# A hybrid decoder layer on one core: the sample's NSA attention moves into the block of the NSA merge, and the scan's decay product moves to GpSimd

## The reference

```python
cum = jnp.cumsum(dt * a, axis=2)
seg = cum_t[..., :, None] - cum_t[..., None, :]
decay = jnp.exp(jnp.where(causal, seg, -jnp.inf))
cb = jnp.einsum('bcign,bcjgn->bcgij', cm, bm)
xdt = xh * dt[..., None]
y_diag = jnp.einsum('bcgeij,bcjgep->bcigep', cb[:, :, :, None] * decay, xdt)
states = jnp.einsum('bcjgn,bcjgep->bcgepn', bm, xdt * decay_end[..., None])
```

```python
s_s = jnp.einsum('bqkgd,bkqmd->bkgqm', qb, k_sel) * scale     # likewise s_c (compressed), s_w (window)
p_s = masked_softmax(s_s, ...)
o_s = jnp.einsum('bkgqm,bkqmd->bqkgd', p_s, v_sel)
o_nsa = (gb[..., 0:1] * o_c + gb[..., 1:2] * o_s + gb[..., 2:3] * o_w) @ w['w_nsa_o']
mixed = gm[:, :, 0] * o_ssd + gm[:, :, 1] * o_nsa + gm[:, :, 2] * o_mem
```

## Time and profile before

| | |
|---|---|
| median of 3 runs | 1879.28 us |
| profiled execution | 1881.37 us, span 1879.4 us |
| mean granted TensorE clock | 0.951 |
| TensorE busy | 1697.0 us (90%) |
| VectorE busy | 949.1 us (51%) |
| ScalarE busy | 704.8 us (38%) |
| GpSimd busy | 662.6 us (35%) |

### The profile page before, as it was taken

One profiled execution on the slowest core, in us unless ns is written; L12 is line 12 of the kernel. 1 busy time (PEld: TensorE's weight loads), 2 busy tenths in 40 slices (PEclk: granted clock), 3 DMA queues, 4 the chain that ended last, 5 costly groups with the idle time before them and its releaser, 6 DMA issues. The chain is left out here.

```text
span 1879.4 us, 33817 instructions
## 1 busy us (share of the span) xinstructions
PE 1697.0 (90%) x13060; PEld 1542.2 (82%) x13060; DVE 949.1 (51%) x1543; ACT 704.8 (38%) x1502; POOL 662.6 (35%) x346
## 2 busy tenths in 40 slices
PE   6999995786997999879997799989998799999999
PEld 5999993455997999536665699988797799999999
DVE  4476766996611352157773313552223568777300
ACT  3333336884611331145551233333412333333221
POOL 2344434663343333125441243011143244444443
PEclk9999998888999999879998899999998899999999
DMA  4223216442222432230003323644423222232233
GB/s 141 69 89 91 95 60 211 169 145 101 79 90 70 147 103 94 94 108 28 1 0 96 118 91 113 225 135 168 180 89 124 61 86 89 91 95 93 70 93 119
DMA packets 60239, 193.65 MB, mean 103 GB/s; under 512 B 6934, under 2 KB 19734, under 8 KB 56726
## 3 DMA queue, kind: packets, MB, share of 16 engines
q1 hardware_dynamic: 58838, 190.30, 30.5%
q10 hardware_dynamic: 1312, 2.14, 0.3%
HBM read 174.47 MB, written 22.14 MB: 105 GB/s over the span
## 5 line engine op out<-in xcount | busy, mean ns | idle before, releaser
L254 POOL TENSOR_TENSOR mm_ring<-mm_raw,mm_ring 128x1024 fp32r<-128x1024 f32 x94 | 229.0, 2438 | 487.9 <-ACT mm_ring L231 364.2
L264 PE MATMUL up_pp<-h,mm_ring 128*128 128x260 f32 x2016 | 244.0, 284 | 3.0 <-POOL mm_ring L254 3.0
L264 PEld LDWEIGHTS up_pp<-h,mm_ring 128*128 128x128 f32 x2016 | 243.8, 189 | 3.2 <-ACT up_conv_s L2850 3.2
L231 ACT CAST mm_ring<-mm_raw 128x1024 fp32r<-128x1024 f32 x106 | 111.1, 1049 | 335.1 <-PE up_pp L264 231.0
L264 PE MATMUL ssd_pp<-h,ssd_ring 128*128 128x260 f32 x1920 | 233.8, 285 | 3.0 <-POOL ssd_ring L254 3.0
L264 PEld LDWEIGHTS ssd_pp<-h,ssd_ring 128*128 128x128 f32 x1920 | 233.2, 190 | 3.2 <-ACT gates_raw L515 3.2
L264 PE MATMUL up_pp<-act_t,mm_ring 128*128 128x260 f32 x1344 | 165.7, 286 | 7.5 <-POOL mm_ring L254 7.5
L264 PEld LDWEIGHTS up_pp<-act_t,mm_ring 128*128 128x128 f32 x1344 | 165.3, 192 | 7.9 <-issue 7.9
L254 POOL TENSOR_TENSOR ssd_ring<-mixed,ssd_ring 128x1024 fp32r<-128x1024 f32 x42 | 102.4, 2440 | 170.0 <-ACT ssd_ring L231 153.6
L264 PE MATMUL nq_pp<-h,nq_ring 128*128 128x260 f32 x960 | 122.5, 289 | 10.4 <-POOL nq_ring L254 10.4
L264 PEld LDWEIGHTS nq_pp<-h,nq_ring 128*128 128x128 f32 x960 | 119.5, 192 | 11.3 <-issue 10.5
(11 more groups left out here) (424 smaller groups left out, 3103.3 us busy)
## 6 DMA issues: line engine op xcount, KB each, us to landing
mm_raw<-in_w_up SPq DMA_DIRECT2D x44, 512.0 KB, 3.7
mixed<-in_w_ssd SPq DMA_DIRECT2D x42, 512.0 KB, 3.5
mem_ring<-in_mem_kv SPq DMA_DIRECT2D x16, 1024.0 KB, 6.0
ms_raw<-in_w_ssd_merge SPq DMA_DIRECT2D x24, 512.0 KB, 3.5
mm_raw<-in_w_mkv_qm SPq DMA_DIRECT2D x24, 512.0 KB, 3.7
nq_raw<-in_w_qk SPq DMA_DIRECT2D x20, 512.0 KB, 3.7
sc_seg<-cum_rows SPq DMA_DIRECT2D x16, 512.0 KB, 4.9
mixed<-in_ssd_state SPq DMA_DIRECT2D x16, 512.0 KB, 4.2
```

The costliest lines, as they stand in the source:

```text
L231: act.copy(self.ring[:, b % 2, 0], self.raw[:, b % 2]).then_inc(self.high, 1)
L254: pool.tensor_tensor(self.ring[:, u, 1], self.raw[:, u], self.ring[:, u, 0].bitcast(F32), ALU.subtract).then_inc(self.low, 1)
L264: last = pe.matmul(out(n), self.ring[:, b % 2, wn, k], x[:, xn, chunk + k, part], start=start and k == 0 and wn + xn == 0, stop=stop and k ...
```

## The change

**Scan.** The step size dt goes into the exponent: log_dt_cum = ln(max(dt, 2e-38)) - cum takes the place of minus cum as the bias, at the price of a logarithm on ScalarE and one more instruction on VectorE, each once, in the projection before the scan. The eight scaled copies of x become one plain copy (sc_xt), and C times B is copied to SBUF beside B turned. GpSimd forms m from SBUF (mix). TensorE waits for GpSimd before the products with m, and SP waits for GpSimd before it reloads sc_seg.

The diff, cut to its core:

```diff
@@ StepSizes.dve_all / act_d
-        do(dve.tensor_scalar(negcum[:], cum[:], -1.0, None, ALU.mult))
+        do(dve.tensor_scalar(log_dt_cum[:], dtr[:], TINY, None, ALU.max))
...
+        do(dve.tensor_tensor(log_dt_cum[:], log_dt_cum[:], cum[:], ALU.subtract))
...
-        act.activation(self.dend[:], self.dend[:], ACT.Exp).then_inc(self.exped, 1)
+        act.activation(self.dend[:], self.dend[:], ACT.Exp)
+        act.activation(self.log_dt_cum[:], self.log_dt_cum[:], ACT.Ln).then_inc(self.exped, 1)
@@ scan, SP
-                    sp.wait_ge(ready, v + 1)
+                    sp.wait_ge(mixed_up, v + 1)
                     load_rows(v + AHEAD)
@@ scan, GpSimd
+            def mix(v):
+                pool.wait_ge(taken, v + 1)
+                pool.wait_ge(exped, v + 1)
+                if v >= 2:
+                    pool.wait_ge(multiplied, v - 1)
+                pool.tensor_tensor(m[:, v % 2], seg[:, v % AHEAD], br[:, v % 2, 0, :].unsqueeze(1).broadcast_to(
+                    [P, HPG, P]), ALU.mult).then_inc(mixed_up, 1)
...
             diagonals(1)
+            mix(0)
             for v in range(STEPS):
                 if v:
                     gate(v - 1)
                 scale(v)
+                if v + 1 < STEPS:
+                    mix(v + 1)
                 if v + 2 < STEPS:
                     hide_future(v + 2)
@@ scan, TensorE
                 if v:
                     pe.wait_ge(gained, v)
+                pe.wait_ge(mixed_up, v + 1)
                 for e in range(HPG):
-                    mm = pe.matmul(pyd[:, e, :], m[:, v % 2, e, :], xdt[:, v % 2, e, :], start=True, stop=True)
+                    mm = pe.matmul(pyd[:, e, :], m[:, v % 2, e, :], xt[:, v % 2, e, :], start=True, stop=True)
@@ scan, ScalarE
-                act.copy(br[:, v % 2, :], pcb[:, 1, :])
-                for e in range(HPG):
-                    ins = act.activation(xdt[:, v % 2, e, :], px[:, e, :], ACT.Copy,
-                                         scale=dtr[:, k, g * HPG + e:g * HPG + e + 1])
-                ins.then_inc(taken, 1)
+                act.copy(br[:, v % 2], pcb[:, 0:2, :])
+                act.copy(xt[:, v % 2], px[:]).then_inc(taken, 1)
@@ scan, VectorE
                 dve.wait_ge(taken, v + 1)
-                dve.tensor_tensor(xend[:, v % 2], px[:], of_heads(wend, v), ALU.mult)
-                dve.wait_ge(exped, v + 1)
-                dve.tensor_tensor(m[:, v % 2], seg[:, v % AHEAD], pcb[:, 0, :].unsqueeze(1).broadcast_to(
-                    [P, HPG, P]), ALU.mult).then_inc(ready, 1)
+                dve.tensor_tensor(xend[:, v % 2], px[:], of_heads(wend, v), ALU.mult).then_inc(ready, 1)
@@ merge_nsa, SP
+            piece(2)
+            sp.wait_ge(scored, 1)
+            keys(0)
+            piece(3)
+            keys(1)
+            piece(4)
+            sp.wait_ge(valued, 1)
+            values(0)
+            piece(5)
+            values(1)
+            for q in range(6, KC + 2):
+                piece(q)
+                if q == 7:
+                    sp.wait_ge(valued, 2)
+                if q >= KC:
+                    part = slice((q - KC) * HALF_K, (q - KC + 1) * HALF_K)
+                    sp.dma_start(mem[:, part], d["mem"][:, part]).then_inc(mem_landed, 16)
@@ merge_nsa, TensorE
+            def gates(t):
+                if t:
+                    pe.wait_ge(gated, t)
+                w.multiply(pe, t // 2, t % 2, lambda m: banks[:, gate_banks(t) + m, 0:HALF], h, 0, HALF_PARTS)
+            def scores(b):
+                if b:
+                    pe.wait_ge(k_landed, 32)
+                pe.wait_ge(q_ready, b + 1)
+                for n in range(2):
+                    for ch in range(2):
+                        for strip in range(STRIPS):
+                            q = 2 * strip + n
+                            mm = pe.matmul(psc[STRIP * strip:STRIP * (strip + 1), 0:PAST + 1], qd[:, ch, q, :],
+                                           kt[:, ch, q, :], start=n == 0 and ch == 0, stop=n == 1 and ch == 1, ...)
...
+            scores(0)
+            gates(0)
...
+            turn_weights(0)
+            gates(1)
+            values(0)
+            scores(1)
+            gates(2)
+            turn_weights(1)
+            gates(3)
+            values(1)
...
+            gates(4)
+            pe.wait_ge(o_done, 1)
+            pe.transpose(pot, osum[:], ident[:]).then_inc(o_turned, 1)
+            for t in range(PLAIN + 1, KC):
+                gates(t)
+            pe.wait_ge(low, KC + 1)
+            for t in range(KC):
...
@@ merge_nsa, ScalarE and GpSimd, end of the block
-            following.write_first_ahead(act)
+            following.write_first_after(act, w)
...
+            for b in range(2):
+                following.write_low_of(pool, 0, b)
@@ build_layer
-                    w = SplitWeights(s, "mn", d["w_nsa_merge"], rings_of=Ring(mn_raw, mn_ring))
+                w_nsa, w_mem, w_merge, w_out = (SplitWeights(s, n, d[x], rings_of=rings) for n, x in (
+                    ("mn", "w_nsa_merge"), ("mp", "w_mkv_qm"), ("mm", "w_mem_merge"), ("po", "w_out")))
```

628 lines of the change are left out of this document (334 added, 294 removed).

## The result

The changed kernel takes 1822.64 us in the median of four runs (1821.56 to 1824.36), before in the same session 1879.08; the ratio is 0.9701, with a 95% interval of 0.9688 to 0.9715. That is 56.4 us less, where 55.3 (1824) was forecast. Its profiled execution took 1823.51 us with a span of 1821.7, so the two traces lie 57.7 us apart.

| TensorE reaches (us from the span's start) | before | after | ahead by |
|---|---|---|---|
| the second group of the first projection | 40.68 | 38.89 | 1.8 |
| the SSD merge, behind the scan | 453.33 | 433.98 | 19.4 |
| the prompt's attention | 816.65 | 797.87 | 18.8 |
| the end of its last matmul | 997.74 | 981.13 | 16.6 |
| the memory projection, behind the NSA merge | 1159.64 | 1102.17 | 57.5 |

What follows compares the result with a forecast made beforehand. VectorE bound the scan; TensorE bounded most else but idled 26 us around the merge's sample attention. Scan 18.6 plus merge 38.1 made 56.7 us less, so 1824 us; own range 1816 to 1832, outer 1812 to 1844.

Steps and rivals of the forecast that it cites:

- Scan, the product off VectorE (15.8 us): Scan loop: one product fewer on VectorE in each of 14 steps, 1.13 us each, 15.8 us saved.
- Scan, the start (2.75 us): Scan start: the second product and its wait for ScalarE's exponentials leave VectorE, 1.62 + 1.13 = 2.75 us saved.
- GpSimd level at 8.05 against 7.99: Scan step: GpSimd with the product at 2.31 us takes 8.05 us, VectorE without it 7.99; called level.
- Rival 2: Scan bound by GpSimd: no reserve, each 0.1 us per step beyond 3 us of cover costs 1.4; to 1840; chance 0.11.
- Scores and values at 1.85 us: Merge, sample attention: each group of 32 records in four strips takes 1.85 us, the first 3.7 at half clock.
- rival 1: Merge: strips do not overlap, scores and values cost as before, 24 us more, 1848; chance 0.08.
- A full drain: Merge, TensorE: eight tiling-mode changes each waiting for the group before would add 1.3 us; weighed, not counted.
- Pieces, small matmuls and evacuations: Merge: sixteen weight pieces 91.8 us, first one cold 1.5 more, small matmuls 4.5, evacuation waits 3.
- Lead-in (6.4) and end (4.8 + 1.5): Merge: 6.4 us before the first scores; 4.8 us from last output piece to next stage, 1.5 for cold start.
- Rivals 3 and 4: Merge: loads and weights late, 5 to 12 us, chance 0.12; or ScalarE's queue makes it slower than before, 0.03.
- held by take_low: Merge: VectorE's take_low could hold GpSimd's subtraction by up to its own length.
- rival 4: Merge: casts refilling the ring queue late on ScalarE; each us of excess costs 14 us over 14 pieces; chance 0.03.

Runs made afterwards that it cites:

- the filler: Kernel with three merge edits, plus one unread matmul on TensorE in the first scan step of each later head group; 1812.66 us, ratio 0.9638.
- The other two pairs of traces: Kernel before against the scan's part alone (1862.70 us), and the merge's part alone (1840.64 us) against the changed kernel.
- the run with the strips in turn: Changed kernel with each group's score and value matmuls ordered all four of one strip, then the next strip; 1833.40 us, ratio 0.9756.
- the run with the later casts: Changed kernel with ScalarE doing each cast of the merge's pieces 2 to 15 four times instead of once; 1832.40 us, ratio 0.9741.

## Why the prediction was right

- *Scan, the product off VectorE (15.8 us).* The step is 7.99 as forecast, but the fourteen steps gave 14.9 us (126.45 to 111.56 between the second step's state update and the last's). The missing 0.9 are waits at the changes of group, 1.36 and 0.44 us over a step of 7.28, where the kernel before had one of 0.86 (9.27 for 8.41). Without the waits on both sides the steps give 15.8, so the product's price was right and the sum lacked the waits. The larger one comes with TensorE at its 1.2 GHz level after a pause, and it is gone with the filler. The other two pairs of traces put the scan's whole gain at 16.0 and 16.3 us, so of the forecast 18.6 between 1.0 and 2.6 us were too much.
- *Scan, the start (2.75 us).* 3.0 by the trace (the second step's state update at 302.86 for 307.61, less the 1.8).
- *GpSimd level at 8.05 against 7.99.* 8.01 and 7.99. The product's pitch is 2.32 us; the mask, of the same shape and with its inputs in the same places, was the right row to take it from. Rival 2 lies close: 0.6 us more on GpSimd in each step shows in the scan's trace (4.2 us), at less than the 6 to 9 that I priced it.
- *Scores and values at 1.85 us.* 1.93 and 1.94, first one 3.65 for 3.7; rival 1 is refuted, and the run with the strips in turn shows that this hung on the order in which they are written. A full drain, which the prediction weighed, doesn't show: the gate behind the strips begins at 1008.89, before the modelled end of their row (1007.02 + 1.94 = 1008.96). That overlap is 0.07 us against the 0.16 between full-width pieces, so by these rows eight changes cost 0.7 us, where the rule of the Trainium skill, "TensorEngine Tiling (Array Packing)", "Key Properties", would have made it 1.3.
- *Pieces, small matmuls and evacuations.* From the first scores to the last output piece (987.29 to 1098.15) 110.9 us, forecast 3.7 + 5.6 + 91.8 + 1.5 + 4.5 + 3 = 110.1. The evacuation waits are 0.46, 0.68, 0.78 and 0.79, 2.7 for the 3 assumed.
- *Lead-in (6.4) and end (4.8 + 1.5).* 5.1 us from the table load to the first scores, since the small copies took less than 0.25 each, and 4.02 at the end. The cold start did come (12.93 for the first 96 matmuls, 12.00 before), but behind the boundary at which I had drawn the sum. So the merge gave 40.9 us less 0.9, where 38.1 was forecast.
- *Rivals 3 and 4.* No gate or output tile of the changed kernel waits for GpSimd or for a DMA. GpSimd's subtraction was held by take_low, as the prediction allowed:

```profile
1016.67 4.09 POOL L257 TENSOR_TENSOR mm_ring<-mm_raw,mm_ring 128x1024 fp32r<-128x1024 f32 x1 [7.96 <-ACT mm_ring L234]
1023.50 2.36 POOL L257 TENSOR_TENSOR mm_ring<-mm_raw,mm_ring 128x1024 fp32r<-128x1024 f32 x1 [2.73 <-ACT mm_ring L234]
```

  4.09 us beside four take_low of VectorE, 2.36 alone; the refill had the room for it. In rival 4 the mechanism stands and its price falls to about a half.

The mechanism was right in both parts, and the total was right to 1.4 us partly by luck. In this pair of traces errors cancel: 1.0 too much for the scan and 0.66 not seen before the prompt's attention, against 1.9 too little for the merge. Two differences that belong to the execution cancel as well, 1.8 us gained at the start and 2.2 lost in the prompt's attention.

## What to carry to other kernels

Where an instruction goes to another engine, ask of the target not only how long it takes but where its inputs lie: the same product added nothing to the step on GpSimd, 1.13 us on VectorE with an input in PSUM, and 2.6 on VectorE from SBUF beside a busy GpSimd. Work that waits on itself (score, exponential, turn, value) can be written between matmul tiles of a later stage, and what stays then is the two ends of the block, each of which can be trimmed by itself. In a ring of two slots, as in the run with the later casts, a late refill is paid in every second piece.

## What the hardware showed that was not expected

- Four column strips overlap to the full only if neighbouring matmuls in the queue go to different strips: 1.93 us for 32 records in turn round the strips, 4.59 strip by strip, where only four records at each change of strip run beside others.
- A pause of 1.78 us in TensorE, in a stretch where it is otherwise busy for most of the time, was followed by matmuls at half speed (3.04 for 2.00, 2.02 for 1.08) at one change of group and by none at the next; with one more matmul of 1.0 us in each pause the granted clock was 1.00 at all three, in one trace.
- VectorE's product with two SBUF inputs took 2.65 us beside a busy GpSimd and 1.21 beside an idle one, and GpSimd's two diagonals 2.16 instead of 1.20.
